# Pads in SBUF: where the moving tensors of a weight stream lie relative to the weights

## What is computed

```python
for l in range(DEPTH):                       # first block; the second is alike
    h = rmsnorm(x, norm_mix_pre[l])
    proj = h @ w_in[l]                       # 1024 x 7168
    ...
    merged = gates[0] * y_ret + gates[1] * y_sc + gates[2] * y_cf
    x = x + rmsnorm(merged @ w_o[l], norm_mix_post[l])
    h = rmsnorm(x, norm_ffn_pre[l])
    up = causal_dwconv(h @ w_up[l], ffn_conv_w[l])        # 1024 x 5632
    gate, val = jnp.split(up, 2, axis=-1)
    f = (jax.nn.silu(gate) * val) @ w_down[l]             # 2816 x 1024
    x = x + rmsnorm(f, norm_ffn_post[l])
```

## Time and profile before

| | |
|---|---|
| median of three runs | 1851.85 us |
| the profiled execution | 1855.75 us |
| its span, first to last instruction | 1854.0 us |
| PE busy | 1801.3 us, 97% |
| DVE busy | 1359.8 us, 73% |
| ACT busy | 1072.8 us, 58% |
| HBM over the span | 168 GB/s |

### The profile page before, as it was taken

How to read it: one execution, slowest core, us unless ns; L and a number is a source line. 1 busy time by engine, 2 the same in 40 slices (tenths; PEclk the granted TensorE clock), 3 DMA queues, 4 the chain that set the end, 5 groups by cost and what they waited for, 6 DMA issues and landing times.

```text
span 1854.0 us, 36333 instructions
## 1 busy us (share of the span) xinstructions
PE 1801.3 (97%) x14784; PEld 1755.3 (95%) x14784; DVE 1359.8 (73%) x2385; ACT 1072.8 (58%) x1808; POOL 190.5 (10%) x200
## 2 busy tenths in 40 slices
PE   8999999999999999999999999999999998999998
PEld 8899999999999999999999889999999998899998
DVE  6898779867889779876768867655567696676553
ACT  5455566655455657654776675544458757655442
POOL 1012410001002410001201003000002100020000
PEclk9999999999999999999999999999999999999999
DMA  8545536664645536663646634565645563346552
GB/s 283 166 158 182 182 118 209 194 209 136 201 161 180 182 126 208 194 208 131 191 148 171 196 103 153 172 197 185 204 161 168 160 201 121 114 148 208 190 184 101
DMA packets 90343, 320.08 MB, mean 173 GB/s; under 512 B 10529, under 2 KB 12993, under 8 KB 90049
## 3 DMA queue, kind: packets, MB, share of 16 engines
q1 hardware_dynamic: 90176, 317.75, 52.8%
HBM read 310.60 MB, written 1.08 MB: 168 GB/s over the span
## 4 chain that ended last, share of the span: by engine, by line
PE 80%; DVE 10%; ACT 4%; issue 3%; POOL 1%; DMA 1%; SPq 0%; DVEq 0%; ACTq 0%; POOLq 0%
PE big L587 74%; PE small L587 5%; DVE L L1109 2%; PE small L586 1%; ACT H L1885 1%; DVE POOL L1466 1%; DVE POOL L1298 1%; DVE POOL L1664 1%; ACT POOL L2269 1%; POOL POOL L2481 1%; ACT POOL L2307 1%; DVE gates L1353 0%; POOL POOL L2460 0%; DVE POOL L1305 0%; PE small L590 0%
## 5 line engine op out<-in xcount | busy, mean ns | idle before, releaser
L587 PE MATMUL big<-HH,H 128*128 128x256 f32 x3344 | 947.3, 283 | 8.2 <-DVE gates L1353 3.5
L587 PE MATMUL big<-HL,H 128*128 128x256 f32 x3344 | 933.1, 279 | 3.9 <-DVE HL L1244 3.8
L587 PE MATMUL big<-HH,L 128*128 128x256 f32 x3344 | 931.6, 279 | 0.0
L1109 DVE TENSOR_TENSOR L<-F,H 128x1024 fp32r<-128x1024 f32 x574 | 702.5, 1232 | 212.5 <-ACT H L1885 211.2
L1885 ACT ACTIVATE H<-F 128x1024 fp32r<-128x1024 f32 x582 | 610.3, 1054 | 212.6 <-PE big L587 208.8
L587 PEld LDWEIGHTS big<-HH,H 128*128 128x128 f32 x3344 | 630.9, 189 | 13.2 <-issue 5.8
L587 PEld LDWEIGHTS big<-HL,H 128*128 128x128 f32 x3344 | 633.1, 189 | 7.8 <-DVE HL L1244 5.9
L587 PEld LDWEIGHTS big<-HH,L 128*128 128x128 f32 x3344 | 632.1, 189 | 0.0
L587 PE MATMUL big<-FH,H 128*128 128x256 f32 x848 | 240.1, 283 | 0.0
L587 PE MATMUL big<-FL,H 128*128 128x256 f32 x848 | 236.2, 279 | 0.0
L587 PE MATMUL big<-FH,L 128*128 128x256 f32 x848 | 236.2, 279 | 0.0
(11 more groups left out here) (237 smaller groups left out, 1795.4 us busy)
## 6 DMA issues: line engine op xcount, KB each, us to landing
F<-in_stream SPq DMA_DIRECT2D x582, 512.0 KB, 4.1
POOL<-POOL SPq DMA_DIRECT2D x32, 128.0 KB, 4.0
POOL<-head_rows SPq DMA_DIRECT2D x8, 256.0 KB, 5.1
X<-in_x SPq DMA_DIRECT2D x2, 512.0 KB, 4.3
POOL<-POOL SPq DMA_DIRECT2D x16, 64.0 KB, 3.0
out_x<-X SPq DMA_DIRECT2D x1, 1024.0 KB, 4.0
POOL<-in_decay SPq DMA_DIRECT2D x1, 768.0 KB, 11.2
POOL<-POOL SPq DMA_DIRECT2D x8, 96.0 KB, 5.2
```

Source lines behind the costliest of these rows:

```text
L587: return pe.e.matmul(out_, lhsT, rhs, start=start, stop=stop)
L1109: v.tensor_tensor(L[:, j % NR, :], F[:, j % NF, :], H[:, j % NR, :].bitcast(F32), ALU.subtract).then_inc(s_lo, 1)
```

## The change

Three pads. `apart` grows from 48 to 92 columns; a pad of 20 columns comes behind FL, ahead of PR; a pad of 44 columns comes behind POOL, ahead of gates and ffn. The description says that the moving tensors of the stream then lie 112 bytes, modulo 256, behind the weights' places instead of 192. No instruction is changed.

```diff
         X = sb("X", [P, KT, T])
-        sb("apart", [P, 48])
+        sb("apart", [P, 92])
         HH = sb("HH", [P, KT, T], F32R)
         HL = sb("HL", [P, KT, T], F32R)
         FHa = sb("FH", [P, 14, T], F32R)
         FLa = sb("FL", [P, 14, T], F32R)
+        sb("apart_back", [P, 20])
         PR = sb("PR", [P, pn])
         CO = sb("CO", [P, cn])
         SCR = sb("SCR", [P, 194])
         POOL = sb("POOL", [P, NPOOL * T])
 
+        sb("apart_tail", [P, 44])
         with nc.sbuf_tensor("gates", [P, 16 * T], F32) as gates:
             pass
         ffn = sb("ffn", [P, 16, T], F32R)
```

## The result

The changed kernel takes 1890.14 us (median of six runs, 1888.08 to 1893.02) against 1856.27 us (six runs, 1845.34 to 1868.60) of the kernel before: ratio 1.0197, 95% interval 1.0162 to 1.0233. It is slower, by 34 us of the medians; the interval excludes no change and reaches from 1.6% to 2.3%. Its profiled execution took 1888.64 us, 32.9 more than that of before. Two things stand out already in the times: the level rose, and the spread shrank from 23 us to 5. All ratios here are of undisturbed executions, each against runs of the kernel before in the same session; left out are two of the kernel before (1871.83 and 1875.69 us) and one at offset 224, which took 6362.39 us.

What follows compares the result with a forecast made beforehand. PE's matmul stream was taken to bound the kernel: 1855.75 us profiled plus 59 for one more step, less 1 hidden, is 1913.8, or 1909.9 against the median, so 1910; range 1880 to 1930, for 8 in 10 1820 to 1980.

Steps and rivals of the forecast that it cites:

- What bounds the kernel: PE, busy 97% of the span; a nanosecond on each product of the matmul stream is a nanosecond on the end.
- The addresses: Tensors start at multiples of 32 bytes, so pads give 128 for 12,576 products and 160 for 768, not 112.
- where 16 bytes do: Rival that the pad gives 128 and 160 instead of 112; held as certain, mattering only where 16 bytes matter.
- DVE and ACT on moved tensors: Instructions of these engines on the tensors at new addresses; priced at nothing.
- The present mix: Stream before: 8,148 products at the lower level, 5,196 at the upper, a mean of 1.39 steps.
- steps: Losses of about 4.4 ns a product, each time moving read and weight load meet, above bare columns plus 2.2 ns.
- The level after: Stream of 13,344 products at the new offset: 2.4 steps, one more than now, 59 us; chance 0.30.
- even trend: Meetings change evenly with offset: 3 to 4 steps at the token form's 64, 1 to 2 at 192, 128 half way.
- its signs: What would show the forecast: four long pieces at 122.2 ns a product, 182 us for 1488 and 193 for 1583.
- What hides: PE waits only a few us on any one producer, so 1 us of the added stream time is taken off.
- The rival by the rule: Two independent ports, so the offset costs nothing: 1852 us, between 1829 and 1888; chance 0.27.
- Without effect, only restarts decide: Same two-port rival: the state at each restart of the stream sets its level, not the offset; chance 0.27.

Runs made afterwards that it cites:

- the run with the other tensors alone: Kernel before with PR, CO, SCR, POOL, gates and ffn at the changed kernel's addresses, HH, HL, FH and FL left at 192: ratio 0.9965.
- the run at 64: Kernel before with HH, HL, FH and FL 64 bytes behind the weights, the rest at the addresses of before: ratio 1.0090.
- everything at 112: Kernel before with HH, HL, FH, FL and ffn exactly 112 behind the weights' places, by longer tensors used from their 16th byte on: 1841.38 us, ratio 0.9907.
- the run with the same distance at other addresses: Kernel before with a 48-column pad ahead of F, moving weights and moving tensors together by 192 bytes, offset still 192: ratio 1.0009.

## Why the prediction was right, and where it was not

**What bounds the kernel: right.** 13,344 products, each 3.6 ns longer (115.2 to 118.8 over all unbroken spacings), are 48 us. The 288 token products, priced at 1.3 us either way, took 230.1 ns before and 232.4 after, 0.7 us.

**The addresses: right, and worth more than the prediction made of it.** 128 and 160 are what the built program of the changed kernel has (HH at 71168, ffn at 209184). The rival said it matters "where 16 bytes do". They do: the kernels at 112 and 128 that differ in one start column are 24 in a thousand apart.

**DVE and ACT on moved tensors, at nothing: right.** 1233 and 1054 ns, and the run with the other tensors alone is not slower.

**The present mix: right.** 1.39 steps were taken; the mean of all spacings before, 115.2 ns, is 1.42.

**The level after: right in sign and nearly in size, for a reason that fell.** Forecast were 2.4 steps, measured are 2.2 (118.7 less 106.7 less 2.2, by 4.45), so the term was 59 us and measured 48. But it was obtained from an even trend between the token form's 64 and the 192 of the stream, and the run at 64 has 117.8, in places 113.3, where the trend wants 122 to 127. The token form's extra steps are its own affair, as the prediction had allowed: with its moving side at 64 (before), 128 (changed) and 192 (the kernel with the stream at 64) it takes 230, 232 and 234 ns, and doesn't fall with the offset. That the interpolation hit was luck. Nor do whole steps hold: 118.7 lies between two, as five unequal spacings. Eleven steps in five products fit the sum; nothing here shows that this is more than arithmetic. The prediction also contradicts itself here: its signs ask for 122.2 ns in the long pieces, 182 and 193 us, which is a step above the upper level, while the 2.4 steps that it summed are 119.5 ns, 178 and 189 us. Measured are 176.6 and 187.9; the signs were wrong and the sum nearly right.

**What hides: wrong.** 1 us was taken off; it was about 15. Of 48 us more in the stream, 32.9 arrived in the profiled executions. The rest is waits that got shorter and a clock that was lower for less time. The waits shrank because ACT's and DVE's chains beside the stream take as long as before while the stream before each rendezvous takes longer. The largest is one in the first layer. The timeline of PE before:

```profile
74.36 0.28 PE L587 MATMUL big<-HH,L 128*128 128x256 f32 x1
76.93 1.62 PE L587 MATMUL small<-POOL 128*128 128x256 f32 x4 [2.30 <-DVE POOL L1426]
78.20 0.56 PE L587 MATMUL big<-HH,H 128*128 128x256 f32 x1
78.56 0.41 PE L587 MATMUL big<-HL,H 128*128 128x256 f32 x1
78.77 0.41 PE L587 MATMUL big<-HH,L 128*128 128x256 f32 x1
```

and of the changed kernel at the same place:

```profile
76.58 0.28 PE L589 MATMUL big<-HH,L 128*128 128x256 f32 x1
76.80 0.92 PE L589 MATMUL small<-POOL 128*128 128x256 f32 x4
77.47 0.37 PE L589 MATMUL big<-HH,H 128*128 128x256 f32 x1
77.68 0.28 PE L589 MATMUL big<-HL,H 128*128 128x256 f32 x1
```

The first product of the next group starts at 78.20 us before and at 77.47 after: by 77 us the slower stream is ahead, for it never had to wait for DVE's line 1426. The wait cost more than its 2.3 us: the matmuls behind it stand 0.21 us apart, as at the 1.2 GHz level, not 0.11. The window shows the clock, before and after:

```profile
74.00:82.00 8.00, 5.70 (x34) 5.32 (x32) 7.15 (x14) 1.45 (x2) 0.00 (x0) 0.79 0.52 167
...
74.00:82.00 8.00, 8.00 (x65) 7.75 (x64) 7.88 (x16) 3.03 (x5) 0.00 (x0) 1.00 0.55 176
```

PE's idle time before its instructions, summed over its groups, falls from 47.8 to 41.0 us, 7 less. The mean granted clock over the span rises from 0.996 to 1.000, and 0.4% of 1854 us is 7 us of full clock, part of it lost while PE was idle anyway. The two together are at most 14 of the 15 us; I have not taken them further apart. A wait does not bring the lower clock with it each time: with everything at 112, PE is busy for 6.38 of the 8 us of this window, and the clock stays at 1.00. The same mechanism works against the fast kernel, which waits more: the one with everything at 112 has 52.8 us of idle time before PE's instructions.

**The rival by the rule: fell.** "TensorE: Matmul & The Clock Gate" (Part 2) of the Trainium skill has the weights' load and the moving read on two independent ports, and "SBUF — State Buffer" (Who interferes with whom) has PE wait on nobody. By that, the kernels at 112 and 128 would take the same time; they differ by 24 in a thousand, with one start column changed. The time of a load and matmul pair is not independent of where its two operands lie; that it is the two reads that meet fits, and is not seen directly. That page's sentence is on other engines; no run here shows PE slowed by another engine's access, and none tested it.

**"Without effect, only restarts decide": half right.** At 192 they do (the same piece is high in one kernel and low in another of the same offset), and at 64 the same two levels occur. At 128, 112 and 0 every long piece of a kind has one level; at 128 the short pieces have two, 118.7 and 120.0.

## What to carry to other kernels

Where a kernel is a stream of weight load and matmul in pairs, read the spacing of starts, and compare the same piece of work across layers: here, two levels at one clock went with a dependence on the places of the two operands, and a pad is a cheap experiment. Check the addresses in the built program, not the sizes in the code; here a rounding to 32 bytes turned a gain of 0.9% into a loss of 2%, and a slice of a longer tensor puts a tensor at the 16 bytes in between. Don't interpolate between two offsets: measure each one, over several restarts, for an offset can have two levels.

## What the hardware showed that was not expected

- The time of a product of 128x128 weights with 256 float32 columns (in the fp32r form) depends on the distance between the two operands in a partition: 113.3, 118.7 or 120.0 ns in long pieces at 112, 128 and 0 bytes modulo 256. 16 bytes suffice for 5.4 ns. 128 and 384 agree, so a period of 256 fits; it was tested at this one pair alone.
- At 192 there are two levels, 113.3 and 117.8 ns. Each holds for over 1500 products without a slip, and which one comes is settled where the stream restarts. The same two occur at 64, mostly the upper one. At 128 short pieces stand at 118.7 or at 120.0, the level of offset 0.
- No bank or line was identified. That the two reads meet is supported by the run with the same distance at other addresses; how they do, and why 112 is good, stays open.
